# Other distances between the operands of the matmuls in SBUF: two larger pads, and the gated parts as two tensors

## The reference, cut to what matters

```
u = causal_depthwise_conv(h @ w_up, conv_w, conv_b)      # first net; 3 taps
a, b = split(u, 2)
y = (gelu(a) * b) @ w_down
# second block's nets, twice:
a, g = split(x @ w_up, 2)
g = causal_depthwise_conv(g, conv_w) + conv_b
y = (gelu(g) * a) @ w_down
```

## Time and profile before

| | us |
|---|---|
| median of 3 runs | 1266.45 (1266.42 to 1271.71) |
| the profiled execution's own time | 1264.75 |
| its span (first to last instruction) | 1263.4 |
| TensorE matmuls busy | 1221.4 (97%) |
| TensorE weight loads busy | 1120.7 |
| VectorE busy | 901.2 |
| ScalarE busy | 609.1 |
| GpSimd busy | 107.8 |

### The profile page before, as it was taken

How to read it: one execution, slowest core, us unless ns; L and a number is a source line. 1 busy time by engine, 2 the same in 40 slices (tenths; PEclk the granted TensorE clock), 3 DMA queues, 4 the chain that set the end, 5 groups by cost and what they waited for, 6 DMA issues and landing times. The chain is left out here.

```text
span 1263.4 us, 21186 instructions
## 1 busy us (share of the span) xinstructions
PE 1221.4 (97%) x8525; PEld 1120.7 (89%) x8528; DVE 901.2 (71%) x1266; ACT 609.1 (48%) x919; POOL 107.8 (9%) x148
## 2 busy tenths in 40 slices
PE   8999999989999999999998999999999999999997
PEld 5888888979999999899988999998987898999996
DVE  5977996675767888845778666767665589666677
ACT  2252123453755666634664555554423464645552
POOL 3893000003000000010000000000200000000000
PEclk9999999999999999999999999999999799999999
DMA  9553444526726667625334456667455105555560
GB/s 278 175 153 108 133 134 143 194 88 195 244 89 200 211 223 228 206 69 160 109 101 167 157 177 229 198 231 167 101 163 185 33 1 174 193 177 191 191 208 35
DMA packets 178734, 202.76 MB, mean 160 GB/s; under 512 B 21884, under 2 KB 163163, under 8 KB 178636
## 3 DMA queue, kind: packets, MB, share of 16 engines
q1 hardware_dynamic: 175083, 191.49, 47.6%
q0 software_dynamic: 3184, 9.77, 2.6%
q10 hardware_dynamic: 369, 0.13, 0.1%
HBM read 200.30 MB, written 1.08 MB: 159 GB/s over the span
## 5 line engine op out<-in xcount | busy, mean ns | idle before, releaser
L1480 DVE TENSOR_TENSOR w_parts<-raw,w_parts 128x1024 fp32r<-128x1024 f32 (+1 forms) x242 | 294.9, 1219 | 131.7 <-ACT w_parts L1469 126.3
L1763 PEld LDWEIGHTS ps<-hT_parts,w_parts 128*128 128x128 f32 x2880 | 342.8, 188 | 2.3
L1763 PE MATMUL ps<-hT_parts,w_parts 128*128 128x256 f32 x2880 | 344.5, 280 | 0.0
L1469 ACT CAST w_parts<-raw 128x1024 fp32r<-128x1024 f32 (+1 forms) x242 | 253.1, 1046 | 166.2 <-PE ps L1763 64.5
L1782 PE MATMUL ps<-w_parts,gT_parts 128*128 128x512 f32 x720 | 173.5, 395 | 1.1 <-DVE w_parts L1480 1.1
L1782 PEld LDWEIGHTS ps<-w_parts,gT_parts 128*128 128x128 f32 x720 | 133.1, 187 | 32.4 <-DVE w_parts L1480 1.3
L478 PE MATMUL ps<-hT,ring 128*128 128x256 f32 x448 | 100.3, 384 | 1.2 <-DVE hT L321 1.2
L1533 PE MATMUL ps<-hT_parts,w_parts 128*128 128x256 f32 x816 | 99.3, 281 | 2.2 <-DVE w_parts L1480 1.6
L1533 PEld LDWEIGHTS ps<-hT_parts,w_parts 128*128 128x128 f32 x816 | 97.0, 188 | 2.9 <-DVE w_parts L1480 1.8
L478 PEld LDWEIGHTS ps<-hT,ring 128*128 128x128 f32 x448 | 85.7, 193 | 14.4 <-issue 1.6
L1887 DVE SCALAR_TENSOR_TENSOR arena_late<-ps,vecT,arena_late 128x255 f32<-128x255 f32 (+1 forms) x176 | 84.9, 482 | 10.5 <-ACT arena_late L1837 4.2
(11 more groups left out here) (413 smaller groups left out, 1564.4 us busy)
## 6 DMA issues: line engine op xcount, KB each, us to landing
raw<-in_ffn_w_up SPq DMA_DIRECT2D x44, 1024.0 KB, 5.1
raw<-in_f_w_up SPq DMA_DIRECT2D x22, 1024.0 KB, 5.2
raw<-in_ffn_w_down SPq DMA_DIRECT2D x22, 1024.0 KB, 5.0
ring<-in_w_in SPq DMA_DIRECT2D x18, 1024.0 KB, 5.8
raw<-in_ev_w_in SPq DMA_DIRECT2D x15, 1024.0 KB, 5.4
raw<-in_f_w_down SPq DMA_DIRECT2D x11, 1024.0 KB, 4.9
ring<-in_x_wkv SPq DMA_DIRECT2D x8, 1024.0 KB, 5.6
ring<-in_w_out SPq DMA_DIRECT2D x4, 1024.0 KB, 8.1
```

The lines of the kernel that those rows point to most:

```text
L1469: self.done(A, A.copy(high[:, c], self.raw[:, u % RAW, c]), self.s_hi)
L1480: self.done(V, V.tensor_tensor(low[:, c], self.raw[:, u % RAW, c], high[:, c].bitcast(F32), ALU.subtract), self.s_lo)
L1763: mm = T.matmul(self.ps[:, b, m * 256:m * 256 + 256], w[:, kk, m * P:(m + 1) * P], x[:, kk, :], start=kk == 0 and q == 0, stop=kk == KD - ...
```

## The change

The pad ahead of hT_parts grows from 1 line (64 bytes) to 7 (448 bytes). gT_parts becomes two tensors, g0T_parts and g1T_parts, each with a pad ahead of it, of 3 and 2 lines; the three places that index it follow. The pad ahead of the arena grows from 1 to 2 lines, and the arena loses 256 columns at its end. In bytes from the start of w_parts, hT_parts now begins at 32768 + 448, g0T_parts at 49152 + 640, g1T_parts at 53248 + 768, the arena at 57344 + 896. `arena_cols` sets where the bias tables begin (`self.bt_at`, at the arena's end) and how much of the arena may be used. No instruction, wait or order is changed.

```diff
--- before.py
+++ after.py
@@ -1269,11 +1269,14 @@
         self.raw = self.sb("raw", [P, RAW, SLOT])
 
         self.w2p = self.sb("w_parts", [P, 2, 2, SLOT], F32R)
-        self.sb("pad_x", [P, LINE])
+        self.sb("pad_x", [P, 7 * LINE])
         self.hTr = self.sb("hT_parts", [P, 2, KD, SEQ], F32R)[:, :, :, :]
-        self.gTr = self.sb("gT_parts", [P, 2, 2, 2, SEQ], F32R)
-        self.sb("pad_arena", [P, LINE])
-        self.arena_cols = 26624
+        self.gTr = []
+        for i, pad in enumerate((3, 2)):
+            self.sb(f"pad_g{i}", [P, pad * LINE])
+            self.gTr.append(self.sb(f"g{i}T_parts", [P, 2, 2, SEQ], F32R))
+        self.sb("pad_arena", [P, 2 * LINE])
+        self.arena_cols = 26624 - 256
 
         self.over = {}
         for at in (4096, 8192, 12288, 16384):
@@ -1776,7 +1779,7 @@
 
     def pe_down_bank(self, i, tt, hf, stop=False):
         wh, wl = (shaped(a, (2, D)) for a in self.parts_of(self.ff["d", i]))
-        gh, gl = self.gTr[:, i % 2, 0], self.gTr[:, i % 2, 1]
+        gh, gl = self.gTr[i % 2][:, 0], self.gTr[i % 2][:, 1]
         for m in range(2):
             for q, (g, w) in enumerate(((gh, wh), (gh, wl), (gl, wh))):
                 mm = self.T.matmul(self.ps[:, 2 * tt + hf, :], g[:, m, tt * P:(tt + 1) * P], w[:, m, hf * 512:(hf + 1) * 512],
@@ -1860,7 +1863,7 @@
             self.A.wait_ge(*self.s_prod.next("A"))
         else:
             self.A.wait_ge(*self.drained(self.ff_fills["b", i]))
-        self.done(self.A, self.A.copy(self.gTr[:, i % 2, 0], self.g32[i % 2]), self.s_ghi)
+        self.done(self.A, self.A.copy(self.gTr[i % 2][:, 0], self.g32[i % 2]), self.s_ghi)
 
     def dve_ffn(self, cols, out):
         self.dve_freed(out[WAY_OUT[1]])
@@ -1906,7 +1909,7 @@
             ins = V.tensor_tensor(g, y[0], self.bank2(fb), ALU.mult)
             self.drain(V, ins, fb)
         V.wait_ge(*self.s_ghi.next("V"))
-        self.done(V, V.tensor_tensor(self.gTr[:, p, 1], g, self.gTr[:, p, 0].bitcast(F32), ALU.subtract), self.s_g)
+        self.done(V, V.tensor_tensor(self.gTr[p][:, 1], g, self.gTr[p][:, 0].bitcast(F32), ALU.subtract), self.s_g)
```

## The result

| | before, us | after, us |
|---|---|---|
| median | 1266.88 (9 runs, 1265.0 to 1271.71) | 1261.62 (9 runs, 1257.58 to 1263.09) |
| profiled execution | 1264.75 | 1257.58 |
| its span | 1263.4 | 1256.3 |
| TensorE matmuls busy | 1221.4 | 1214.3 |

The ratio is 0.995, 95% interval 0.9933 to 0.9966: 5.3 us faster. I had forecast 1252, 14.6 us faster. The diff adds three lines, so L1763 is now L1766, L1533 L1536, L1782 L1785, L2176 L2179, L1729 L1732, L1535 L1538.

A forecast was written before the change was run, and what follows sets the result against it. The prediction took the kernel to be bound by TensorE's matmul rate. Its terms, -15.0 + 1.8 - 1.0 - 1.4 + 1.0 = -14.6 us, gave 1250.2 from the profiled 1264.75, or 1252 us against the median; range 1244 to 1269.

The forecast's parts named there:

- What bounds the kernel: Whole kernel: bound by the rate at which TensorE takes its matmuls, busy 1221.4 of 1263.4 us.
- part 1: L1763 and L1533, activation parts moved: 90% of 3696 matmuls go from 117.8 to 113.3 ns, -15.0 us.
- Part 4: L1782, gated buffers at +640 and +768 bytes from the slots: 231.3 ns per matmul, -1.4 us.
- parts 1 and 2: Activation step both ways: moving activations gain 15.0 us, 636 matmuls with moving weights from slots lose 1.8 us.
- Arena parts: Loops with arena parts, moved 448 bytes past the activation parts: 708 matmuls, fast share rises to 0.62, -1.0 us.
- Part 6: Steady iterations shrink to 16.4 us, other engines still fit; +1.0 us over the kernel for splits that land late.
- Rival 1: Steady loops stay at 117.8 ns, as a stream's start sets the pace, not addresses: 1266 us, chance 0.29.
- Rival 2: L1782: new gated gaps meet the weight load a second time, +4.8 us, kernel slower at 1273 us, chance 0.11.

The follow-up runs named there:

- the second trace of the changed kernel: The changed kernel run again with nothing changed, on the chip of two other runs: 0.9947 of before, 1261.09 us.
- The streams alone: Two runs of a separate kernel with only TensorE's streams on constant data, operand distances varied; up products took 113.3 to some 120 ns each.

## Why the prediction was wrong

- **What bounds the kernel** was right: TensorE's pace; none of the long waits in the trace after grew by more than 0.4 us. The five loops fell by 5.1 us in the profiled pair (5.0 + 2.0 + 0.1 + 1.0 - 3.0), and by 6.4 against the second trace of the changed kernel; the medians moved by 5.3. The profiled pair lies 7.2 us apart; groups outside the five loops moved by up to 1.6 us either way.
- **The failed step is part 1's "all or nothing ... I take 90%"**, the term of 15.0 us, which measured 5.0. I took it that a steady loop, having no break, would stay in the fast pace. The runs show that the down between two up streams hands a pace on: in steady running fast behind a down with the gated parts at 2 or 3 lines modulo 4, slow behind 0, alternating behind 1, with the two exceptions told above (the down behind L1705, and the iterations behind a halt). The changed kernel has a 2 and a 0, so over half of its steady iterations are slow, and L1766 fell by 4.2 us where 11.7 of the 15.0 were its share. I had treated parts 1 and 4 as independent; they are one. With both gated buffers at 11 lines L1766 falls by 9.6 us, most of its share, and the kernel stands at 0.9903 of before, 12 us, near the 14.6 that the sum gave.
- **A smaller part of the same term stays open.** The 816 products of L1536 were to give 3.3 us (90% of 816 x 4.5 ns) and gave 0.8; at 11 lines they gave 0.9. They don't stand behind a down of the steady loop, so the gated distances don't explain it, and no run shows what does.
- **The exchange of distances** (parts 1 and 2) was right in its direction. Moving weights from slots lost 3.0 us in the profiled run, about 1.4 of them by the lower clock; in the second trace of the changed kernel they lost 1.6, with 1.8 forecast. Arena parts gained 1.0, as forecast.
- **Part 4** had the downs at 231.3 ns in the mean of both buffers, -1.4 us; measured are 232 and 227.5, and -2.0. That they differ between the two buffers, and what this hands on, I did not see.
- **Part 6**: the 1.0 us for late splits showed in the first net, whose fast stretches are longer than the second's (the row below, 11.22 us for 96 instead of 11.05), half a microsecond in its three. The mechanism was right, as the halt for the split in the kernel at 11 lines shows, and it has a second price that I had not seen: behind a halt the pace is open again.

```profile
420.22 11.22 PE L1766 MATMUL ps<-hT_parts,w_parts 128*128 128x256 f32 x96
```

- **Rival 1** (addresses don't matter, the start decides) had a true half: at one distance both paces occur. The streams alone refute the rest. The Trainium skill's page "SBUF — State Buffer", section "Who interferes with whom", gives TensorE two independent read ports and says that it never waits on anyone. With TensorE alone at work, the pace of one loop moved between 113.3 and 120 ns by the distance of its two operands. So the traces don't agree with the rule, and the measurement decides; which read waits is not shown.
- **Rival 2** did not occur: the downs with g0T_parts are below 233.3 ns.

## What to carry to other kernels

Where float32r products of 256 columns follow each other without a gap, put the tensor that moves 64 bytes short of a multiple of 256 behind the one that is loaded as weights, and look at the pace from start to start, not at the busy share: here it was 113.3 instead of 117.8 or 120 ns. A stream of another shape between two such streams has a distance of its own to choose, and has to be chosen for the pace that it hands on as well as for its own: 11 lines, not the best for the downs themselves, gave the best sum. Try such layouts on streams alone first; two runs of that kind gave the whole table, and the undisturbed steady loops of the full kernel agreed with it. What they leave out is what comes in between there: a halt for a late split, or a short stream of another kind.

## What was not expected of the hardware

- The time of a product depends on the distance of its operands modulo 256 bytes: for 256 columns 120, 117.8, 118.6 and 113.3 ns at 0, 64, 128 and 192 bytes; for 512 columns 227, 233.4, 232.4 and 228.9.
- At 192 bytes there are two lasting paces, 113.3 and 117.8 ns, and a stream without a halt kept the one that it began with. Why 192 bytes can be fast and the others cannot, and which read waits for which, these runs don't show.
- Open as well: in the kernel before, single units of L1763 and L1533 were fast at a distance of 64 bytes. With the streams alone none at that distance was.
